# A streaming encoder layer on one core: products of one-hot rows written to every fourth word of PSUM

## The reference

```
q = (tb @ wq).reshape(tokens, 8, 2, 128)
s = einsum("thid,hikd->thik", q, keys)          # 2 x 128 scores per head
sv, si = top_k(s, 16)                           # 16 best of each half
comb = sv[:, :, 0, :, None] + sv[:, :, 1, None, :]
fv, fi = top_k(comb, 16)                        # 16 best pairs: expert = key1 * 128 + key2
w = softmax(fv)
act = gelu(einsum("thkd,td->thk", u[eidx], tb))
out = einsum("thk,thkd->td", w * act, v[eidx])
```

## Time and profile before

| | us |
|---|---|
| three runs | 5761.89, 5723.29, 5736.1 (median 5736.1) |
| profiled execution | 5734.65 |
| its span in the trace | 5732.9 |
| gates, from the first copy of keys to the end of the last eviction | 3344.28 to 3636.43 |
| first work of the experts phase | 3651.94 |

### The profile page before, as it was taken

The page is one execution under the profiler, slowest core; times in us unless marked ns, Lnnn a source line. Parts: engine busy times, 40 slices in busy tenths (PEclk is TensorE's granted clock), DMA queues, the critical chain, the costliest instruction groups (busy, mean ns, idle before and its releaser), DMA issues. The chain is left out here.

```text
span 5732.9 us, 83257 instructions
## 1 busy us (share of the span) xinstructions
PE 4712.3 (82%) x28607; PEld 4320.5 (75%) x28607; DVE 3661.4 (64%) x6858; ACT 1812.0 (32%) x3649; POOL 1507.0 (26%) x1356
## 2 busy tenths in 40 slices
PE   5899999956665686988498746699999999999995
PEld 4899999944444444887387645688999998999994
DVE  2100035556666343223469977699999999999997
ACT  0111123323332233111144358533333333333332
POOL 0000000001111000000000000266777767777763
PEclk8999999978777566999799879899999999999998
DMA  2233222222211312334299713699999999999995
GB/s 97 99 115 114 96 82 92 101 78 98 89 72 73 59 25 61 126 121 157 94 374 339 264 63 143 249 357 346 352 372 366 357 363 360 354 364 371 356 356 209
DMA packets 342330, 1169.80 MB, mean 204 GB/s; under 512 B 40544, under 2 KB 85728, under 8 KB 337504
## 3 DMA queue, kind: packets, MB, share of 16 engines
q0 software_dynamic: 147456, 536.94, 25.3%
q1 hardware_dynamic: 156672, 483.22, 24.1%
q10 hardware_dynamic: 38112, 148.52, 6.8%
HBM read 971.35 MB, written 197.46 MB: 204 GB/s over the span
## 5 line engine op out<-in xcount | busy, mean ns | idle before, releaser
L1888 POOL DMA_INDIRECT ex_ur<-scr_u_rows,ex_at x512 | 614.4, 1200 | 320.5 <-DVE ex_ur L2065 146.4
L1890 POOL DMA_INDIRECT ex_vr<-in_expert_v,ex_at x512 | 614.2, 1200 | 265.7 <-issue 145.9
L2073 DVE SCALAR_TENSOR_TENSOR ex_acc_rows<-ex_vr,ex_wt,ex_acc_rows 128x1024 f32<-128x1024 f32 x512 | 649.6, 1279 | 38.7 <-ACT ex_wt L1993 37.3
L2065 DVE SCALAR_TENSOR_TENSOR ex_ur<-ex_ur,h_rows 128x1024 f32<-128x1024 f32 x512 | 619.1, 1218 | 2.9 <-DMA ex_ur<-scr_u_rows,ex_at 2.9
L1882 POOL COPY ex_at<-picked_at 128x4 uint32 x128 | 79.6, 622 | 1833.1 <-POOLq L117 1832.6
L803 POOL TENSOR_TENSOR sd_cts<-sd_cT,sd_ea 128x512 f32<-128x512 f32 x72 | 93.3, 1295 | 1726.0 <-ACT sd_ea L768 1726.0
L395 DVE TENSOR_TENSOR pr_w_lo<-pr_w,pr_w_hi 128x1024 fp32r<-128x1024 f32 x74 | 90.7, 1225 | 689.8 <-ACT pr_w_hi L391 689.8
L1900 PE MATMUL ex_ps<-hd_hi,ex_u_hi 128*128 128x320 f32 x2048 | 469.7, 311 | 28.4 <-DVE ex_u_lo L2039 25.8
L1900 PE MATMUL ex_ps<-hd_lo,ex_u_hi 128*128 128x320 f32 x2048 | 467.4, 309 | 0.0
L1900 PE MATMUL ex_ps<-hd_hi,ex_u_lo 128*128 128x320 f32 x2048 | 467.4, 309 | 0.0
L1991 ACT ACTIVATE ex_gel<-ex_dot 128x1 f32<-128x1 f32 x512 | 103.9, 203 | 983.4 <-DVE ex_ur L2065 983.4
(11 more groups left out here) (356 smaller groups left out, 11055.5 us busy)
## 6 DMA issues: line engine op xcount, KB each, us to landing
pk_raw_u<-in_expert_u SPq DMA_DIRECT2D x128, 512.0 KB, 6.4
scr_u_rows<-pk_rows_u ACTq DMA_DIRECT2D x128, 512.0 KB, 6.2
ex_u<-in_expert_u SPq DMA_DIRECT2D x128, 512.0 KB, 6.9
ex_v<-in_expert_v SPq DMA_DIRECT2D x128, 512.0 KB, 9.8
scr_gate<-gt_stage SPq DMA_DIRECT2D x10, 4096.0 KB, 11.2
ex_gate<-scr_gate SPq DMA_DIRECT2D x32, 1280.0 KB, 13.1
pr_w<-in_w_main SPq DMA_DIRECT2D x74, 512.0 KB, 4.7
scr_plain<-pr_out ACTq DMA_DIRECT2D x42, 576.0 KB, 3.1
```

Source lines behind the costliest of these rows:

```text
L1888: nc.gpsimd.indirect_dma_start(out=ur[:, s], out_offset=None, in_=scr["u_rows"], in_offset=by).then_inc(ur_in[s], 16)
L1890: nc.gpsimd.indirect_dma_start(out=vr[:, s], out_offset=None, in_=io["expert_v"].rearrange("j i d -> (j i) d"), in_offset=by).then_inc(vr_ ...
L2065: v.scalar_tensor_tensor(out=ur[:, s], in0=ur[:, s], scalar=1.0, in1=rows[:, s], op0=ALU.mult, op1=ALU.mult, accum_out=dot[:, m:m + 1]).th ...
L2073: v.scalar_tensor_tensor(out=acc_g[:, s], in0=vr[:, s], scalar=wt[:, m:m + 1], in1=acc_g[:, s], op0=ALU.mult, op1=ALU.add).then_inc(row_r[ ...
```

## The change

PSUM for one place is now `[2, 128, 4]`: token group g (one bank each), key, token in the group. So a product writes its 128 columns to every fourth word of a bank. The eviction goes over (key, g, token in group): it reads runs of 4 words, from the two banks in turn, and writes runs of 8 words (32 bytes) to `stage`, whose layout is as before. Nothing changes in the number of instructions or elements of TensorE and ScalarE.

On VectorE the wait ahead of the copy of keys asks for the products up to the end of the half before the last one, `t * US + (h - 1) * (US // 2)`, and no longer for those of the last one; that half is the last whose products and scalings read `cur[:, h]`. In the very first half it is left out, for which the first turn stands ahead of the loop and the loop runs over the other four.

```diff
-        ps = pb("gt_ps", [P, 2, B * P])
+        ps = pb("gt_ps", [P, 2, B // 4, P, 4])
...
-            with dve.Fori(0, DT) as t:
+            def turn(t, first):
...
                     dve.wait_ge(mm[s], u + START)
                     if at == 0:
-                        for e in range(S):
-                            dve.wait_ge(mm[e], t * US + h * (US // 2) + START)
+                        if not first or h == 1:
+                            for e in range(S):
+                                dve.wait_ge(mm[e], t * US + (h - 1) * (US // 2) + START)
                         v.tensor_copy(cur[:, h], picks[:, :, ds(t * P + h * HALF, HALF)]).then_inc(cur_r[h], 1)
...
+            turn(0, True)
+            with dve.Fori(1, DT) as t:
+                turn(t, False)
...
-                        last = nc.tensor.matmul(ps[:, s % 2, b * P:(b + 1) * P], one1[:, s, b], one2[:, s, b], start=True, stop=True)
+                        last = nc.tensor.matmul(ps[:, s % 2, b // 4, :, b % 4], one1[:, s, b], one2[:, s, b], start=True, stop=True)
...
-                nc.scalar.copy(stage[:, h, :, at:at + B].rearrange("p k t -> p t k"), ps[:, j % 2].rearrange("p (t k) -> p t k", t=B)).then_inc(ev[j % 2], 1)
+                nc.scalar.copy(stage[:, h, :, at:at + B].rearrange("p k (g t) -> p k g t", t=4), ps[:, j % 2].rearrange("p g k t -> p k g t")).then_inc(ev[j % 2], 1)
```

## The result

The changed kernel's four runs have a median of 5641.16 us (5634.64 to 5656.94), those of before 5729.69: ratio 0.9844, interval [0.9812, 0.9876], 88.5 us less. Two more comparisons of the same two programs gave 0.9868 [0.9841, 0.9895] and 0.9882 [0.9863, 0.9901]. They leave out one slow execution of the changed kernel, 8662.46 us at a mean granted clock of 0.53. Over all three, weighted by the changed kernel's runs, the difference of the means is (4 x 90.7 + 5 x 76.3 + 5 x 62.8) / 14 = 76 us.

The account below looks back on a forecast made before the run. ScalarE was taken to bound the gates mid-half, with VectorE's waits stalling the seams; 33 us from seams plus 39 from the eviction, 72, taken from 5734.65 gave 5663 us, own range 5645 to 5680, all cases up to 5735.

Parts of the forecast that it names:

- The wait for keys: VectorE ahead of the copy of keys at half seams: its 7.56 us wait goes, and ScalarE's 32.9 us of idle.
- The eviction: ScalarE's copy from PSUM to stage: 1909 ns falls to 1040, within 1014 to 1909, taking 0.87 us off its batch.
- the second step: In ScalarE's eviction: 1.72 ns an element is two steps for one, the second being the price of writes 256 bytes apart.
- The products: TensorE's writes to every fourth PSUM word: no added time, rows stay 116 ns apart.
- doubled step: In TensorE's products: a lone PSUM word costing two quick steps, 0.91 ns, is hidden entirely by float32's 0.91 ns a column.
- The first rival: TensorE becomes the bound at twice the time, rows 213 to 232 ns: 5720 to 5744 us; chance 0.18.
- the second (0.08): TensorE at four times the time, rows 427 to 464 ns: slower, 5992 to 6041 us; chance 0.08.
- The new bound: VectorE bounds the changed gates phase: 80 batches of 2.64 us, 3.9 of key copies, 4.0 at the end.
- VectorE's jumps: VectorE's four jumps back to the loop's start, no longer hidden by waits: 1 us in all.
- ScalarE's slack: ScalarE's batch in the gates is 2.28 us, below VectorE's 2.64; 31 us of eviction gain become waits for VectorE.
- The sum: Gates phase 220.1 us against 292.15, a gain of 72: 33 from the seams and 39 from the eviction.
- the forecast's case: The whole program at 5663 us, chance 0.60; 0.93 of that counted as faster by over 1%.

Follow-up runs that it names:

- waits_only: Changed kernel without its PSUM layout and new eviction, so only the new wait against the kernel before: ratio 0.9945, gates phase 257.2 us.
- far_writes: Changed kernel with the eviction going token by token, lone words read and written 64 words apart: eviction 1898 ns, gates 272.4 us.
- lone_reads: Changed kernel with PSUM in a row as before; eviction reads lone words 512 bytes apart, writes runs of 8: ratio 0.9859, gates 234.5 us.
- layout_only: Kernel before with only the changed PSUM layout, product and eviction, old wait and loop kept: ratio 0.9929, gates 262.3 us.
- short_gaps: Changed kernel with the one-hot rows in bfloat16, making each product one pass: product rows 194 ns apart.
- six_on_act: Changed kernel with 6 of 8 tokens weighed on ScalarE in place of 5: ratio 0.9845 against the kernel before, gates 232.8 us.

## What of the prediction held, and the step that failed

- **The wait for keys**: 33 us and no stall in its place. waits_only measured 35, and in the changed kernel VectorE's only idle time ahead of a copy of keys is the first one's 6.4 us. Right.
- **The eviction**: 1040 ns forecast, 989 measured (988 to 990 in four kernels). Off by 51 ns, and without effect, since VectorE sets the pace. The reason given, that writes far apart cost the second step, was right; far_writes and lone_reads show it, and layout_only shows the gain apart from the wait. What the prediction did not draw from it is that PSUM need not be touched at all.
- **The products**: no change in 16 rows, 2.02 us. Right. The reason given was that a float32 product gives out its columns slowly enough to hide a doubled step. short_gaps shows the doubling, 194 ns against 100 for a one-pass product, and at clock 0.50 the reason holds in numbers; at the upper level it stays argued. The first rival (0.18) and the second (0.08) are out here. The first was also summed too low: 256 steps at 0.46 ns, doubled, are 236 ns a row, not 213 to 232.
- **The new bound**: 80 x 2.64 + 3.9 + 4.0 = 219.1, measured 218.94. The 1 us for VectorE's jumps was not there. ScalarE's slack was overrated: 0.36 us a batch forecast, about 0.3 by six_on_act (2.64 - 2.35), and 23.2 us of idle time for VectorE in all, 4.2 of them at the phase's start, where 31 were forecast beside those of the start.
- **The sum** for the phase was 72 us and the phase gave 73.2, and 73.1 to 73.4 between any two of the six traces.
- **The step that failed is the difference outside the gates, which the prediction put at nothing, and the range made from that**: "its own range is 5645 to 5680", from the bounds of the jumps and of the eviction and "the scatter of the runs (5723 to 5762)". The bounds of the jumps are worth 1 us downward and those of the eviction next to nothing, since VectorE sets the pace, so about 17 us were left for scatter. The forecast was 5663 and the median of four runs 5641, 22 us lower. 5 us of it are the starting point: the profiled execution's 5734.65, while the four runs of before have a median of 5729.69. 1 us is the phase. The other 15 us, 88.5 - 73.2, lie outside the gates, in code that the change does not touch.
- What the runs show of these 15 us: outside the gates one program's traces differ by up to 37 us (5399.5 to 5436.5), in part with TensorE's granted clock in the attention phase (0.61 and 351.0 us, 0.68 and 336.7 us). Of the 14.5 us by which the two first traces differ there, the attention phase alone has 348.9 - 336.7 = 12.2. The same excess over the phase was 3 us in the second comparison (76.3) and -10 in the third (62.8), and it has both signs in the other kernels. So the 15 us are the luck of two small samples, as far as is known; only one of the four changed executions was traced, and why the other three were quick stays open. Over 14 runs in three comparisons the difference is 76 us, close to the sum; that the remaining 3 us are scatter too is likely and not shown.
- The chance of faster by over 1%, 0.56 with the forecast's case, was on the right side: all three ratios lie beyond it, though the third's interval ends at 0.9901.

## What to carry to other kernels

Where an engine writes with a long stride, turn the loop of that copy so that the writes come in runs, and let the reads do the jumping: from PSUM they cost ScalarE nothing here, and no other engine's layout has to change. A wait that protects a double buffer should ask for the use before the last; the old one here cost 35 of its phase's 292 us. Both gains count only as far as the next engine allows: apart they were 35 and 45 us, together 73, because VectorE became the bound. When an edit acts on 5% of the program, sum it up within its phase, and take the range of the whole from the scatter of what is left, which several traces of one program show.

## What the runs showed of the hardware beyond what was expected

- ScalarE reads lone words 512 bytes apart in PSUM at full speed (988 ns for 1024, against 989 in runs of 4), and writes to SBUF 256 bytes apart at half speed (1898 ns with lone words on both sides, 1909 with a read in a row).
- bfloat16 products that write every fourth word are 194 ns apart and 100 in a row, at clock 0.50; float32 products have 2.02 us for 16 rows in both layouts at clock 1.0, and 13 rows in the same 3 us at 0.50.
- A float32 multiplication of 128 columns on GpSimd took 1315 ns beside a busy VectorE, of 384 columns 1741 ns, and with the latter one of VectorE's two comparisons of 1024 elements went from 1215 to 1793 ns.
- With the pauses of TensorE at the seams gone, its clock over the gates phase went from 0.91 to 0.98. It was 0.98 in waits_only and lone_reads too, and 0.90 in layout_only, which keeps the pauses. TensorE does not set the pace of the changed phase, and the sum does not hang on it.
